# Moving the next scores ahead of half a filler tile in a sparse attention, and reordering the first attention's opening on one Trainium2 core

## The reference

```python
# 16 heads in 2 key groups, head width 64
s_c = einsum(qc, kc) * scale                  # compressed keys (31 per group)
p_c = _masked_softmax(s_c, cmp_end <= t);  o_c = p_c @ vc
s_s = einsum(qc, k_sel) * scale               # selected keys, here all causal ones
p_s = _masked_softmax(s_s, kpos <= t);     o_s = p_s @ v_sel
s_w = einsum(qc, kw) * scale                  # window keys
p_w = _masked_softmax(s_w, mask_w);        o_w = p_w @ vw
return gc[..., 0:1] * o_c + gc[..., 1:2] * o_s + gc[..., 2:3] * o_w
# the first block's first attention ("forgetting"), 8 heads of width 64
log_f = jax.nn.log_sigmoid(fa + b_forget)
c = jnp.cumsum(log_f, axis=1)
s = where(mask, einsum(q_i, k) * scale + c_i - c_keys, NEG_INF)
p = softmax(s);  out = p @ v
```

## Time and profile before

| | |
|---|---|
| median of 3 runs | 2111.0 us (2109.75 to 2113.06) |
| profiled execution, its own time | 2111.81 us |
| its span | 2110.0 us |
| PE busy | 2070.6 us, 98% of the span |
| DVE, ACT, POOL busy | 64%, 48%, 34% |
| granted TensorE clock over the span | 0.997 |
| first attention | its first scores at 99.30 us |
| sparse attention, 32 units | from about 1197 us to 1525 us |

### The profile page before, as it was taken

One profiled execution on the slowest core, in us unless ns is written; L12 is line 12 of the kernel. 1 busy time (PEld: TensorE's weight loads), 2 busy tenths in 40 slices (PEclk: granted clock), 3 DMA queues, 4 the chain that ended last, 5 costly groups with the idle time before them and its releaser, 6 DMA issues.

```text
span 2110.0 us, 31131 instructions
## 1 busy us (share of the span) xinstructions
PE 2070.6 (98%) x10658; PEld 1751.9 (83%) x10658; DVE 1348.5 (64%) x2278; ACT 1015.5 (48%) x1788; POOL 724.8 (34%) x544
## 2 busy tenths in 40 slices
PE   8999999999999999999999999999999999999998
PEld 6778888888988888988887788788878888889886
DVE  6497863667752366674278799899767337676523
ACT  4466663533432353434244577767655325344322
POOL 2133452513333163442337510211165315233331
PEclk9999999999999999999999999999999999999998
DMA  5323263334433243443325322222364533435331
GB/s 174 119 78 105 73 224 99 120 115 158 137 124 98 80 130 130 152 147 110 91 93 171 100 71 96 67 79 85 115 198 133 179 99 120 139 129 169 100 100 60
DMA packets 74320, 251.31 MB, mean 119 GB/s; under 512 B 8265, under 2 KB 8521, under 8 KB 73713
## 3 DMA queue, kind: packets, MB, share of 16 engines
q1 hardware_dynamic: 51120, 182.08, 27.9%
q0 software_dynamic: 11392, 40.72, 5.7%
q10 hardware_dynamic: 11712, 27.27, 3.5%
HBM read 229.57 MB, written 18.89 MB: 118 GB/s over the span
## 4 chain that ended last, share of the span: by engine, by line
PE 86%; DVE 7%; POOL 2%; issue 2%; DMA 2%; ACT 1%; DVEq 0%; SPq 0%; POOLq 0%; ACTq 0%
PE bank L188 25%; PE bank L190 25%; PE bank L189 25%; PE bank L194 3%; PE bank L195 3%; POOL hid L738 2%; PE bank L2160 2%; DVE w_lo L162 1%; DMA w_raw<-stream 1%; DVE xn_lo L608 1%; PE bank L2821 1%; PE bank L920 1%; PE bank L2823 1%; PE bank L2829 1%; DVE squares L237 1%
## 5 line engine op out<-in xcount | busy, mean ns | idle before, releaser
L162 DVE TENSOR_TENSOR w_lo<-w_raw,w_hi 128x1024 fp32r<-128x1024 f32 x337 | 454.5, 1352 | 409.4 <-ACT w_hi L157 406.5
L188 PE MATMUL bank<-xn_hi,w_hi 128*128 128x512 f32 (+1 forms) x1432 | 553.2, 386 | 4.8 <-DVE w_lo L162 3.3
L157 ACT ACTIVATE w_hi<-w_raw 128x1024 fp32r<-128x1024 f32 x337 | 354.8, 1055 | 418.1 <-PE bank L190 250.8
L190 PE MATMUL bank<-xn_hi,w_lo 128*128 128x512 f32 (+1 forms) x1432 | 538.6, 376 | 0.0
L189 PE MATMUL bank<-xn_lo,w_hi 128*128 128x512 f32 (+1 forms) x1432 | 538.6, 376 | 0.0
L188 PEld LDWEIGHTS bank<-xn_hi,w_hi 128*128 128x128 f32 x1432 | 270.6, 189 | 56.7 <-DVE w_lo L162 4.9
L190 PEld LDWEIGHTS bank<-xn_hi,w_lo 128*128 128x128 f32 x1432 | 269.5, 188 | 50.3
L189 PEld LDWEIGHTS bank<-xn_lo,w_hi 128*128 128x128 f32 x1432 | 270.2, 189 | 45.5 <-issue 2.6
L188 PE MATMUL bank<-down_hi,w_hi 128*128 128x512 f32 x528 | 205.8, 390 | 0.0
L190 PE MATMUL bank<-down_hi,w_lo 128*128 128x512 f32 x528 | 205.4, 389 | 0.0
L189 PE MATMUL bank<-down_lo,w_hi 128*128 128x512 f32 x528 | 205.4, 389 | 0.0
(11 more groups left out here) (473 smaller groups left out, 4231.6 us busy)
## 6 DMA issues: line engine op xcount, KB each, us to landing
w_raw<-stream SPq DMA_DIRECT2D x337, 512.0 KB, 3.6
s_raw<-stream POOLq DMA_DIRECT2D x48, 512.0 KB, 6.3
spill_g<-gate_out ACTq DMA_DIRECT2D x16, 256.0 KB, 2.0
m_more<-spill_g POOLq DMA_DIRECT2D x3, 1024.0 KB, 12.9
x<-xt SPq DMA_DIRECT2D x4, 512.0 KB, 7.1
x<-xt ACTq DMA_DIRECT2D x1, 2048.0 KB, 11.1
spill_x<-x ACTq DMA_DIRECT2D x1, 2048.0 KB, 7.5
spill_ga<-ga_out ACTq DMA_DIRECT2D x8, 256.0 KB, 2.6
```

The lines of the kernel that those rows point to most:

```text
L157: nc.scalar.activation(w_hi[:, slot, :], w_raw[:, slot % 2, :], ACT.Copy).then_inc(split_hi, 1)
L162: nc.vector.tensor_tensor(w_lo[:, slot, :], w_raw[:, slot % 2, :], w_hi[:, slot, :], ALU.subtract).then_inc(split_lo, 1)
L188: nc.tensor.matmul(to, a_hi, b_hi, start=start, stop=False, skip_group_check=True)
L190: return nc.tensor.matmul(to, a_lo, b_hi, start=False, stop=stop, skip_group_check=True)
```

## The change

Four edits, and the waits that go with them:

1. Sparse attention, PE: the scores of U + 2 move from behind the filler tile to behind `turn(U, 3)`, ahead of the second half of the tile; the compressed transpose moves between tiles 4 to 5 and 6 to 7 of it. In unit 14 (`keys_change`) the scores stay where they were.
2. Sparse attention, keys of group 1: ACT's `stage_k` is cut in two, set 0 with the compressed keys in unit 14 and set 1 in unit 15; `cross_q(4)` follows the first of them directly. POOL makes the low part of set 1 after the rotation step of that turn.
3. First attention, POOL: the bias goes out for heads 0 and 1 at once and for 2 to 7 after the staging of head 1; head 2 is staged ahead of `vs`.
4. First attention, DVE: `lft_lo` moves ahead of three rotary instructions, and the wait for the other heads' bias moves into the first turn of the loop.

```diff
-            def units_pool(pool, between):
+            def units_pool(pool, between, staged=2):
                 for h in range(HEADS1):
-                    if h + 2 < HEADS1:
+                    if staged <= h + 2 < HEADS1:
                         stage_low(pool, h + 2)
...
                 step(nc.vector.tensor_tensor(rope_t[r, :], rope_t[r, :], rope_s[r, :], ALU.mult))
+                dve.wait_ge(a["lft_hi"], 1)
+                nc.vector.tensor_tensor(lft_lo[:], banks[3][:, 0:32], lft_hi[:], ALU.subtract).then_inc(a["lft_lo"], 1)
...
-                dve.wait_ge(a["lft_hi"], 1)
-                nc.vector.tensor_tensor(lft_lo[:], banks[3][:, 0:32], lft_hi[:], ALU.subtract).then_inc(a["lft_lo"], 1)
...
-                dve.wait_ge(a["cum"], 16)
                 def between_a(dve, h):
+                    if h == 0:
+                        dve.wait_ge(a["cum"], 16)
...
-                for heads, landed in ((slice(0, 1), a["pos"]), (slice(1, 8), a["cum"])):
-                    pool.dma_start(negc[:, heads, :].rearrange("p h s -> p (h s)"),
-                                   cum_d[heads.start * S:heads.stop * S].partition_broadcast(P)).then_inc(landed, 16)
+                def spread(heads):
+                    return pool.dma_start(negc[:, heads, :].rearrange("p h s -> p (h s)"),
+                                          cum_d[heads.start * S:heads.stop * S].partition_broadcast(P))
+                spread(slice(0, 2)).then_inc(a["pos"], 16)
                 a_stage_low(pool, 1)
+                spread(slice(2, 8)).then_inc(a["cum"], 16)
+                a_stage_low(pool, 2)
                 a_stage_v_low(pool, 0)
+                pool.wait_ge(s["v_lo"], 1 + az["v_lo"])
...
-                    fill(slot, range(4, KT)).then_inc(used, 1)
+                    keys_change = U == 14
+                    if U + 2 < UNITS and not keys_change:
+                        score(pe, U + 2)
+                    fill(slot, range(4, 6))
                     if u % 2 == 0:
                         compressed_turn(i, u // 2)
-                    if U + 2 < UNITS:
+                    fill(slot, range(6, KT)).then_inc(used, 1)
+                    if keys_change:
                         score(pe, U + 2)
...
-                def stage_k(g):
-                    at_least(act, s["scored"], 64 * g, z["scored"])
-                    high_kc(g)
-                    high_k(g)
+                def stage_k(g, m):
+                    if m == 0:
+                        at_least(act, s["scored"], 64 * g, z["scored"])
+                        high_kc(g)
+                    high_k(g, (m,))
...
-            def high_k(g):
-                for m in range(2):
+            def high_k(g, sets=(0, 1)):
+                for m in sets:
...
                     highs(U, (0, 1))
+                    if U == 14:
+                        stage_k(1, 0)
+                        cross_q(act, 4)
+                    if U == 15:
+                        stage_k(1, 1)
...
                     highs(U, (2, 3))
-                    if u == 2 and i < 7:
+                    if u == 2 and i < 7 and i != 3:
                         cross_q(act, i + 1)
...
-                        if i == 3:
-                            stage_k(1)
...
-                        low_k(pool, 1, 8)
+                        low_k(pool, 1, 8, (0,))
...
                     if i == 3:
+                        low_k(pool, 1, 8, (1,))
                         low_v(pool, 1)
```

More of the change, by code:

```diff
@@ L1523, in between_a @@
                         pool.wait_ge(a["rope"], ROPE_PARTS)
-                a_pool(pool, between_a)
+                a_pool(pool, between_a, 3)
                 b_stage_low(pool, 0)
@@ L2271, in low_q, with low_k @@
                     pool.wait_ge(s["q_lo"], 2 * i + j + 1)
-            def low_k(pool, g, base):
-                for m in range(2):
+            def low_k(pool, g, base, sets=(0, 1)):
+                for m in sets:
                     k = nqk[:, g + 8 + 2 * m, :]
```

## The result

| | before | after |
|---|---|---|
| median of the runs | 2111.3 us (2109.75 to 2113.06, 4 runs) | 2140.7 us (2140.13 to 2144.54, 4 runs) |
| ratio to before, 95% interval | | 1.0144 (1.0132 to 1.0156) |
| profiled execution, its own time | 2111.81 us | 2140.13 us |
| its span | 2110.0 us | 2138.1 us |
| granted clock over the span | 0.997 | 0.992 |

The change makes the kernel 29.4 us slower where 9.3 were forecast. The direction was right; the measured loss is three times the forecast one and lies outside the range. The first part of the page, which answers to the earlier trace rows, hides it: PE's share is the same 98%, with 15 us more of busy time for the same number of matmuls.

The account below looks back on a forecast made before the run. PE, busy 98% of the span, was taken as the bound, with no waits on its path in steady state. 12.6 + 2.7 - 1.5 + 0.7 - 1.3 - 3.9 = +9.3 us gave 2120.3 us, range 2115 to 2126.

Parts of the forecast that it names:

- The scores of a pair's first unit: Six sparse-attention units: moved scores make PE wait 2.10 us each for the next pair's queries, +12.6 us.
- The hold: Rival, sparse attention: POOL holds DVE's small operation, up to 1.3 us in six units, some 2127 us; chance 0.13.
- Keys: Units 14 and 15: key copies behind the high parts save 2.4 us, a new wait costs 1.1; together -1.3.
- The compressed values: Fourteen sparse-attention units: six matmuls leave 0.19 us of the ACT and DVE chain uncovered each, +2.7 us.
- The tile ends later: Odd sparse-attention units: later filler end delays ACT's table load and bank 3 copy, 0.1 x 7 = +0.7 us.
- Unit 30: Sparse attention: six matmuls now lie between compressed transposes and compressed values, a gain of -1.5 us.
- The first attention: First mixer: earlier lft_lo -1.0, head 1's crossing DMA -2.0, head 2's staging -1.3, DVE some 0.4 late; sum -3.9 us.
- PE did not go around its waits: Rival, sparse attention: PE runs the tile's matmuls while scores wait, removing the 12.6; 2107.7 us, chance 0.05.
- the smaller wait: Rival, sparse attention: only half of the 12.6 us of waits for queries is left, 2114 us; chance 0.08.

Follow-up runs that it names:

- e1: Kernel before with one added PE wait for the queries behind the last transposes of six third units, nothing moved: 2128.6 us, ratio 1.0086.
- e2: Changed kernel with nine unused 512-column matmuls ahead of each of the six waiting scores: 2133.1 us, ratio 1.0104.
- e9: Changed kernel with POOL's rotation held until DVE's small operation on the row maxima is done: 2134.2 us, ratio 1.0109.
- e5: Changed kernel with ACT's cross_q directly behind the first high parts in the third units: 2118.1 us, ratio 1.0030.
- e10: e5 with POOL's rotation also put behind DVE's small operation: 2113.5 us, ratio 1.0009.
- e3: Kernel before with only the move of the scores and compressed transposes: 2140.1 us, ratio 1.0143.
- e6: Kernel before with only the edit on the keys of group 1: 2109.7 us, ratio 0.9988.
- e8: Kernel before with the first attention's edits, the keys' edit and, in unit 30 alone, the earlier compressed transposes: 2105.9 us, ratio 0.9971.
- e4: Kernel before with only the first attention's edits: 2110.1 us, ratio 0.9999.
- e12: e8 with POOL's low parts of head 2's queries waiting until DVE has scaled head 0's probabilities: 2104.1 us, ratio 0.9965.
- e11: Changed kernel with four unused matmuls ahead of each waiting score, in place of the nine of e2: 2134.5 us, ratio 1.0106.

## Why the prediction was wrong

**The step that failed** is "The scores of a pair's first unit": "6 x 2.10 = +12.6 us", with 2.04 and 2.5 as ends. The mechanism, its place and its length were right (12.7 us in the row of waits, 2.11 for one, and e1 has 2.11 per unit at full clock). But a wait was priced at its own length. Of the matmuls behind it the prediction said only that they are the same ones; they were not as fast. Four of six waits were followed by half clock: +8.8 us by the units' lengths, 7.7 by e2. No rival had it. It also does not stand in PE's row of waits, so that "whatever is not in its row of waits costs nothing" is wrong: slower matmuls cost time and count as busy. The rows of before could not price it, since the wait of 1.81 us in the earlier trace rows had full clock behind it. But that is one case, and e1 shows that it happens in some cases of one and the same wait. An open end of the range was missing, not a number. Why one of two equal waits brings the clock down and the other does not is not shown here.

**The hold was a rival and belonged into the sum.** It was given 0.13, and up to 1.3 us in six units. It came true in all six at 1.1 us each at full clock (e9), 6.6 us together: PE waits 0.38 for `npt_lo` (0.75 us by starts, e5 against e10) and the rest lengthens the wait for the queries. With it in the sum the forecast would still have been 13.5 us short, most of it half clock. The argument against it ("DVE has some 0.4 us to spare") took its size down and did not stop it. The Trainium skill, SBUF — State Buffer, section Who interferes with whom, adds which DVE instructions contend with POOL: those with both inputs in SBUF, and the tensor-scalar form in its two-port mode; one with a single SBUF input outside such a mode does not. The trace agrees in unit 14, where POOL works from 1355.08 to 1356.36 and from 1356.44 to 1357.70: the compressed softmax's small scalar operation (0.17 us in unit 6) and its product of two SBUF operands are held until POOL's instruction ends, and its row sum, which has one SBUF input, takes the same 0.29 us as in unit 6, where POOL rests.

```profile
1355.19 0.29 DVE L2524 TENSOR_REDUCE small<-csc 128x4 f32<-128x128 f32 x1
1355.51 0.89 DVE L2525 TENSOR_SCALAR small<-small 128x4 f32<-128x4 f32 x1
...
1356.64 1.09 DVE L2527 TENSOR_TENSOR small<-small,gates 128x4 f32<-128x4 f32 x1
```

**Keys: -1.3 forecast, -0.75 found.** The two units hold more than the keys' edit: the move alone (e3) takes 1.86 us out of them, with no wait left for `npt_lo` or `cpt_lo` in unit 14 and 1.61 us for `cpad`. Put on top of the move, the edit costs 1.1 us: the forecast took its gain from waits of before that the move removes by itself. In the changed kernel unit 14's transposes do not wait for `npt_lo` and its values not for `cpt_lo`, as forecast, but its compressed transposes wait 1.77 us for `cpad`, where "stay or grow to 0.7" was said. In unit 15 there is no wait for POOL's key parts (1.1 forecast); the same small operation is held there for 0.92 us and PE waits for `npt_lo` again. With the old order of PE (e6) the edit gives 2.0 us. The lines are of e3 and then of the changed kernel.

```profile
1361.06 0.66 PE L2176 MATMUL bank<-ident,cpad 128*128 128x128 f32 x4 [1.61 <-DVE cpad L2519]
```
```profile
1358.11 0.65 PE L2182 MATMUL bank<-ident,cpad 128*128 128x128 f32 x4 [1.77 <-DVE cpad L2529]
...
1367.45 0.79 PE L2166 MATMUL bank<-ident,nprob 128*128 128x128 f32 x3 [0.47 <-DVE npt_lo L2500]
```

**The compressed values: right.** 0.19 per unit: e10's third units, with wait and hold gone, are 0.26 longer.

**The tile ends later: 0.7 forecast, 2.9 found.** The place was right and the size was not. In unit 8 PE is through its first transposes before bank 3 is free, for ACT's table load (from 1282.03, 1.28 us) and copy of the old tile end at 1283.93:

```profile
1282.95 0.95 PE L2166 MATMUL bank<-ident,nprob 128*128 128x128 f32 x7
1284.07 0.47 PE L188 MATMUL bank<-xn_hi,w_hi 128*128 128x512 f32 x1 [0.17 <-ACT gr_out L2376]
```
```profile
1283.33 0.60 ACT L2376 ACTIVATE gr_out<-bank 128x512 f32<-128x512 f32 x1
```

The bracket says 0.17, but from the first transposes to the tile's first matmul it is 1.12 us, 0.70 in the same unit before. The unit is 0.6 longer, of which the other 0.19 is the compressed values': 0.4 in each of seven units.

**Unit 30: -1.5 forecast, -0.9 found.** The chain takes longer than 2.01 us there, 2.49, with 0.49 of wait for `cpt_lo`, ahead of which DVE makes a `w_lo` (1.21 us, begun 0.1 us after the transposes) and an `npt_lo`. In e8 the same `w_lo` begins 0.8 us before the transposes, the chain takes 2.01 us and the unit is -1.4.

```profile
1538.27 0.60 PE L2182 MATMUL bank<-ident,cpad 128*128 128x128 f32 x4
...
1540.76 0.50 PE L194 MATMUL bank<-cpt_hi,vcs 128*128 128x512 f32 x1 [0.49 <-DVE cpt_lo L2512]
```

**The first attention: -3.9 forecast, -2.1 at the first feed-forward in the two traces, -1.0 by e4's time.** More traces bear the 2.1 out: in the nine with the new opening the first feed-forward starts at 392.3 to 393.8 us, and in the three with the old one and full clock at 395.4 to 395.7. All three waits of the earlier trace rows went, and head 2's scores start at 115.88 in place of 118.33. A new wait of 0.6 us for a later head's crossing DMA takes a little back. More was lost before that: the prediction had DVE "some 0.4 late", but POOL's work for head 2, moved ahead, held the scaling of head 0 (DVE, POOL and PE of the changed kernel).

```profile
108.13 3.23 DVE L1074 TENSOR_SCALAR prob<-prob,small 128x128 f32<-128x128 f32 x4
```
```profile
107.67 1.28 POOL L984 TENSOR_TENSOR q_rest<-qk_raw,qs_hi 64x512 fp32r<-64x512 f32 x1 [2.70 <-ACT qs_hi L967]
```
```profile
111.42 0.66 PE L920 MATMUL bank<-ident,prob 128*128 128x128 f32 x4 [1.40 <-DVE prob L1074]
...
115.88 0.22 PE L194 MATMUL bank<-ks_hi,qs_hi 128*128 128x128 f32 x1
```

**The sum as the units have it:** six third units at full clock, 6 x 3.37 = 20.2 (holds 6.6, as e9 takes away; compressed values and the rest 1.5, as e10 leaves; waits the other 12.1); half clock 8.8; first units 4.3; unit 0 0.2; keys -0.75; unit 30 -0.9; the rest -0.5. That is 31.3. Less the first attention, and with the scatter between executions, it is the 28.3 us between the two profiled ones. Of the 20.1 us by which the median is above the forecast, the half clock makes 8.8, the holds 6.6, the tile's end 2.2 and the first attention 1.8. PE did not go around its waits: that rival and the smaller wait are refuted by the six waits themselves.

## What to carry to other kernels

A wait of PE in the middle of a dense stretch costs its length and, in part of the cases, a stretch at half clock behind it: here waits of 12.7 us in the row of waits cost 22.6 (e5). When a change adds one, put the second price into the sum or at least into the range, and look whether the producer can be moved first (e5 did that by moving one call). When a change moves POOL's work, write down which DVE instructions then run beside it: a small one on the path can cost most of a POOL operation (1.27 us in place of 0.17 here), and making POOL wait for it cost nothing that the traces of e10 and e12 show. Price the parts of a change in the order of the others, not one by one on the kernel before: the keys' edit gives 2.0 us there and costs 1.1 with the move.

## What the runs showed of the hardware

- Six waits of PE for the queries, by length, and how many of them had half clock in the profiled execution: 1.18 us, 1 (e11); 1.84 us, 3 (e1); 1.85 us, 2 (e9); 2.11 us, 4 (changed kernel) and 5 (e3); with work in the wait, none (e2). Other waits kept full clock: 1.77 us in unit 14, in all seven traces that have it, and 2.14 us in the first attention of e1.
- A DVE operation on 4 values a partition took 0.15 to 0.18 us alone and up to 1.27 us beside a POOL operation of 1.3 us in the changed kernel. Four scalings took 1.28 us alone and 3.23 us beside two POOL operations (1.28 and 1.27 us).
- From the first feed-forward to the sparse attention, where no kernel here differs, the fourteen traces take 799.6 to 803.1 us, so sums over distant landmarks are less sure than distances within a unit.
